# A chosen expert multiplied twice in mid-stage with the same weight pieces, 33 chunks always run

## The chip, the cores and the metric

One core of one Trainium2 chip runs the kernel. The metric is the device time of one execution in microseconds (us); the kernel before takes 1665.71 us, the median of 3 runs (1665.44 to 1667.03). The parts of a core that matter here: TensorE (PE in the profile) multiplies, VectorE (DVE) and ScalarE (ACT) do the elementwise work, GpSimd (POOL) issues gathers, and SyncE (SP) issues every other DMA.

## The reference

Two layers over 512 tokens of 1024 features. Each layer has a mixer (a short convolution in layer 0, sparse attention in layer 1) and then a mixture of experts; the change is in the latter:

```python
g_top = argmax(xf @ w_rg + b_rg)                 # one of 4 groups
e_logits = (xf @ w_re + b_re).reshape(n_tok, 4, 8)
top_vals, top_idx = lax.top_k(e_logits[g_top], 2)
expert = g_top * 8 + top_idx                     # 2 of 32 experts for each token
weights = p_g * softmax(top_vals)
rank = place of the assignment among those of its expert
...
ys = (silu(xc @ w_gate[e]) * (xc @ w_up[e])) @ w_down[e]     # e has 1024x512, 1024x512, 512x1024
out = segment_sum(ys * row_w, row_tok)
```

There are 1024 assignments to 32 experts, so 32 tokens an expert on average; all 32 experts of a layer are used, 6.3 MB of weights each.

## The kernel before

The two expert stages (`experts`, L863) work in chunks of C = 64 tokens of one expert. Chunk c below E = 32 is expert c with its first 64 tokens. An expert with more than 64 gets overflow chunks 32, 33, ...; their number (`novf`) and experts (`ovf_e`) are computed on the chip, and every engine branches on the number after chunk 31 (`overflow`, L1098).

*Weights.* A chunk's weights are 6 pieces of 1 MB: two halves each of gate, up and down (`load_piece`, L433, issued by SP). They lie in a ring of NR = 18 pieces, three chunks. SP loads piece p when the use of piece p - 18 has been counted by the semaphore `s_used` (L1125). Fifteen of the 18 first pieces are prefetched during the stages before, the last three as the first gathered rows land.

*A chunk on TensorE* (`pe_step`, L988): gate-up (`pe_gate_up`, L925), two halves of 16 matmuls, each half after its two pieces have landed; two of the four 128-token tiles of the pair of chunks before, where the weighted results are put back to their tokens by a matmul with a pick matrix (`pe_tile`, L978, `pe_products`, L968); the transpose of the hidden product (L942); the turning of a later pair's rows (`pe_turn`, L915); down (`pe_down`, L952). ACT makes silu (L1013) and y_high (L1021), DVE the hidden product (L1072), y_low (L1051) and the additions into x (L1058). An overflow chunk does all four tiles of what is pending itself, two before the transpose and two before its own down. After the last chunk `end` (L1248) puts back what is left: the pair of chunks 30 and 31 where there was no overflow, the last overflow chunk alone otherwise.

*Tables.* The Router's `vector` ends in `slots` (L762): from the rank and count of every expert it computes the slot (64 x chunk + row) of each assignment. In the expert stage's block `vector_table` (L804) turns slots into one-hot matrices, `tensor_places` (L618) multiplies them into the token list of every chunk, `vector_indices` (L820) makes the gather's indices of it, and `vector_tail` (L830) the weights and the overflow table (`s_table`). The first pair's rows do not wait for this: they have indices of their own (`first_pair`, L750) and are gathered while slots runs.

*Order.* Each engine's queue is in program order. DVE does vector_table, then turns the first rows (`dve_turned`), then vector_indices, vector_tail and the chunks. TensorE turns the first rows, does tensor_places, then the chunks. In chunk 0, after gate-up, it multiplies the weight table (`s_wt`), which SP waits for in layer 1 before it loads the final norm's gain, ahead of piece 18.

Of the kernel before, what the change touches and what calls it, by code (L numbers as in the profile page):

```python
# [59 lines left out]
NCH = E + N_OVF  # L60
# [19 lines left out]
def program(nc, a, out):  # L80
    with ExitStack() as ctx:
# [32 lines left out]
        m.ovf_e = sb("ovf_e", [1, N_OVF + 1], I32)  # L114
        m.banks = ctx.enter_context(nc.psum_tensor("ps", [P, 8, 512], F32))
# [153 lines left out]
def conv_mixer(nc, m, r, hT, u, csb, y):  # L269
# [4 lines left out]
    with ExitStack() as ctx:  # L274
# [9 lines left out]
        rms, rms_row = m.rstd[:, 0, :], sb("c_rms_row", [P, S])  # L284
# [58 lines left out]
        @block.vector  # L343
        def _(dve):
            own = Chain(dve, s_own)

            def roots():
                ms, tmp = m.ss[:, 4:8], m.ss[:, 8:12]
                dve.wait_ge(s_sq, NT)
                dve.tensor_scalar(ms, m.ss[:, 0:4], -0.5 / D, -0.5 * EPS, ALU.mult, ALU.add).then_inc(s_ms, 1)  # L350
                dve.wait_ge(s_rt, 1)
                own.step(dve.reciprocal(rms, rms))

                own.step(dve.tensor_tensor(tmp, rms, rms, ALU.mult))
# [12 lines left out]
            roots()  # L367
            dve.wait_ge(s_row, 1)
            own.step(dve.tensor_copy(rms_row[:], m.ps[6][:]))
            dve.wait_ge(s_cw, 16)  # L370
            for j in range(NK):
                b = j % 2
                dve.wait_ge(s_proj, 3 * j + 1)
                own.step(dve.tensor_tensor(csb[:, b, :], m.ps[3 * b][:], rms_row[:], ALU.mult))
                dve.wait_ge(s_proj, 3 * j + 2)
                own.step(dve.tensor_tensor(csb[:, b, :], csb[:, b, :], m.ps[3 * b + 1][:], ALU.mult))
                own.step(dve.tensor_tensor(u[:, b, 2:], csb[:, b, :], rms_row[:], ALU.mult))
# [5 lines left out]
                own.step(dve.tensor_tensor(y[:, b, :], y[:, b, :], rms_row[:], ALU.mult))  # L383
# [71 lines left out]
class Router:  # L455
# [8 lines left out]
    def __init__(self, nc, m, L, keep, tmp):  # L464
# [13 lines left out]
        self.inc = sb(keep, "inc", [P, E])  # L478
# [17 lines left out]
        self.one, self.base = sb(tmp, "one", [P, E]), sb(tmp, "base", [P, E])  # L496
# [182 lines left out]
    def vector(self, dve):  # L679
# [57 lines left out]
        def constants():  # L737
            own.step(dve.tensor_scalar(self.falling[:], m.iota[:, 0:E], -1.0, 64.0, ALU.mult, ALU.add))
            own.step(dve.memset(self.one[:], -float(C)))
            own.step(dve.tensor_scalar(self.col[:], m.iota[:, 0:NCH], float(C), None, ALU.mult))  # L740
            own.step(dve.tensor_scalar(self.base[:], m.iota[:, 0:E], float(C), None, ALU.mult))
# [20 lines left out]
        def slots():  # L762
# [11 lines left out]
            own.step(dve.scalar_tensor_tensor(out=self.late[:], in0=rank, scalar=float(C) - 0.5, in1=each(begin),  # L774
                                              op0=ALU.is_gt, op1=ALU.mult))
            own.step(dve.tensor_tensor(self.slot[:], rank, each(self.base[:]), ALU.add))
# [53 lines left out]
    def vector_tail(self, dve, own):  # L830
# [11 lines left out]
        own.step(dve.tensor_scalar(self.inc[:], self.inc[:], 1.0 / C, float(1 - E), ALU.mult, ALU.add))  # L842
        own.step(dve.tensor_tensor(self.inc[:], self.inc[:], m.iota[:, 0:E], ALU.add))
# [5 lines left out]
        own.step(dve.tensor_copy(m.ovf_e[:], self.tabf[:]))  # L849
        dve.tensor_copy(m.novf[:], self.inc[0:1, E - 1:E]).then_inc(self.s_table, 1)  # L850
# [12 lines left out]
def experts(nc, m, L, r):  # L863

    with ExitStack() as ctx:
# [32 lines left out]

        def y_place(c):

            return min(c, E - 1) % NY
# [23 lines left out]
        def pe_gate_up(pe, c):  # L925
# [15 lines left out]

# [10 lines left out]
        def pe_down(pe, c):  # L952
# [5 lines left out]
            for h in range(2):  # L958
                p = NPIECE * c + 4 + h
# [138 lines left out]
        def overflow(eng, step, end=None):  # L1098
# [4 lines left out]
            def level(j):  # L1103

                if end:
                    with eng.If(n < j + 1):
                        end(E + j)
                if j < N_OVF:
                    with eng.If(j < n):
                        step(E + j)  # L1110
# [8 lines left out]
        def _(sp):  # L1119
            def step(c):  # L1120
                e = c
                if c >= E:
                    e = sp.value_load(m.ovf_e[0:1, c - E + 1:c - E + 2], min_val=0, max_val=E - 1)
                for p in range(NPIECE * c, NPIECE * (c + 1)):
                    if p >= NR:  # L1125
                        sp.wait_ge(s_used, p - NR + 1)
                        load_piece(sp, m, L, p, e)
# [8 lines left out]
            for c in range(E):  # L1136
                step(c)
# [4 lines left out]
            def end(c):  # L1142
                for n in range(2):
                    sp.wait_ge(s_used, last_use(c, (n,)))
# [15 lines left out]
        def _(act):  # L1160
            for c in range(E):
# [17 lines left out]
        def _(pool):  # L1179
# [4 lines left out]
            for c in range(E):  # L1184
# [11 lines left out]
        def _(dve):  # L1196
# [18 lines left out]
            for c in range(E):  # L1215
# [21 lines left out]
        def _(pe):  # L1237
            for n in range(PAIR):
                pe_turn(pe, n)
            r.tensor_places(pe)  # L1240
            for c in range(E):
                pe_step(pe, c)
# [57 lines left out]
def last_use(c, slots):  # L1300

    return max(p for p in range(NPIECE * c) if ORDER[0][p % NR] in slots) + 1
# [785 lines left out]
```

## Time and profile before

| | |
|---|---|
| median of the runs | 1665.71 us |
| the profiled execution's own time | 1663.04 us |
| its span | 1661.3 us |
| TensorE busy | 1546.8 us, 93% |
| DVE, ACT, POOL busy | 702.1, 308.2, 46.2 us |
| granted TensorE clock, mean | 0.974 |
| moved by DMA | 464.28 MB |
| expert stage of layer 0, of layer 1 | about 259 to 733 us, 1155 to 1655 us |

A line of the profile gives source line, engine, operation, tiles (output <- input), then times. A timeline row is start, duration and count of merged instructions, and in brackets how long the engine stood before it and what released it. "PE clock 1.00" is the full clock, 0.50 half of it. A DMA share of 1 means that all 16 DMA engines were busy.

### The profile page before, as it was taken

How to read it: one execution, taken by the hardware profiler on the slowest of the kernel's cores; microseconds unless marked ns; L12 is line 12 of the kernel's file. 1: busy time of each engine (PE TensorE's matmuls, PEld its weight loads, DVE VectorE, ACT ScalarE, POOL GpSimd, SP SyncE). 2: the span in 40 equal slices, each digit the busy share in tenths (PEclk: the TensorE clock that was granted, in tenths of full speed). 3: DMA queues.
4: the chain of work that ended last, by engine and by line, in shares of the span. 5: the costliest groups of instructions: out<-in, count | busy, mean ns of one | idle time of the engine just before them, and what ended most of it. 6: DMA issues, size and time to landing. Idle time of an engine off the chain costs nothing. (4 is left out here: it accounts for less than half of the span.)

```text
span 1661.3 us, 18728 instructions
## 1 busy us (share of the span) xinstructions
PE 1546.8 (93%) x7356; PEld 725.5 (44%) x7356; DVE 702.1 (42%) x1507; ACT 308.2 (19%) x639; POOL 46.2 (3%) x61
## 2 busy tenths in 40 slices
PE   8999987999999999989999899996999998899995
PEld 4444453444444334345654445554344443433442
DVE  2222344333333233355364599535233333323335
ACT  2000130000000000030333478622000100000002
POOL 0000001000000000000000000000000000000000
PEclk9999998999999999999999999997999999999998
DMA  6271409999999999954310300064999999999993
GB/s 203 76 274 55 169 38 368 418 421 419 420 420 421 420 420 420 419 162 145 102 51 0 152 2 1 10 274 168 383 420 420 420 420 419 421 420 420 420 420 145
DMA packets 112647, 464.28 MB, mean 279 GB/s; under 512 B 29473, under 2 KB 56097, under 8 KB 62625
## 3 DMA queue, kind: packets, MB, share of 16 engines
q1 hardware_dynamic: 107216, 454.52, 68.2%
q0 software_dynamic: 5328, 8.40, 1.4%
q8 instruction: 64, 1.05, 0.3%
q14 instruction: 39, 0.31, 0.1%
HBM read 467.60 MB, written 6.29 MB: 285 GB/s over the span
## 5 line engine op out<-in xcount | busy, mean ns | idle before, releaser
L937 PE MATMUL ps<-raw,e_xT 128*64 128x512 f32 x2080 | 474.5, 604 | 44.3 <-DMA raw<-in_expert_w_up 44.3
L937 PEld LDWEIGHTS ps<-raw,e_xT 128*64 128x64 f32 x2080 | 156.0, 139 | 350.6 <-issue 348.3
L1072 DVE TENSOR_TENSOR e_sg_hid<-e_sg_hid,ps 64x512 f32<-64x512 f32 x65 | 44.3, 681 | 446.9 <-ACT e_sg_hid L1013 446.9
L1058 DVE TENSOR_TENSOR x_res<-x_res,ps 128x512 f32<-128x512 f32 x264 | 168.9, 681 | 3.7 <-PE ps L973 1.6
L407 PE MATMUL ps<-c_hT,raw 128*128 128x512 f32 x384 | 165.2, 592 | 0.4 <-DMA raw<-in_conv_w_in 0.4
L963 PE MATMUL ps<-raw,e_hT 128*64 128x512 f32 x704 | 160.8, 598 | 0.9
L1013 ACT ACTIVATE e_sg_hid<-ps 64x512 f32<-64x512 f32 x65 | 38.6, 593 | 477.8 <-PE ps L937 477.8
L1021 ACT ACTIVATE e_yhi<-ps,e_wtab 128x512 fp32r<-128x512 f32 x65 | 44.7, 687 | 399.4 <-PE ps L963 399.4
L1742 PE MATMUL ps<-a_spare,raw 128*128 128x512 f32 x256 | 115.1, 606 | 3.8 <-DVE a_spare L1503 3.8
L973 PE MATMUL ps<-e_yhi,e_pick 64*128 64x512 f32 x520 | 109.6, 418 | 4.8 <-DVE x_res L1058 3.9
L407 PEld LDWEIGHTS ps<-c_hT,raw 128*128 128x128 f32 x384 | 72.8, 190 | 91.5 <-issue 90.9
L1051 DVE SCALAR_TENSOR_TENSOR e_ylo<-ps,e_wtab,e_yhi 128x512 fp32r<-128x512 f32 x65 | 48.8, 751 | 143.4 <-ACT e_yhi L1021 143.4
L973 PE MATMUL ps<-e_ylo,e_pick 64*128 64x512 f32 x520 | 103.0, 393 | 0.4 <-DVE e_ylo L1051 0.4
L963 PEld LDWEIGHTS ps<-raw,e_hT 128*64 128x64 f32 x704 | 46.6, 136 | 86.6 <-issue 75.4
L973 PEld LDWEIGHTS ps<-e_yhi,e_pick 64*128 64x128 f32 x520 | 48.7, 184 | 66.4 <-issue 52.4
L1742 PEld LDWEIGHTS ps<-a_spare,raw 128*128 128x128 f32 x256 | 49.4, 195 | 63.8 <-issue 63.4
L963 PE MATMUL ps<-e_raw,e_hT 128*64 128x512 f32 x336 | 76.7, 598 | 0.5
L2053 ACT ACTIVATE a_spare<-ps,t_mn 128x128 f32<-128x128 f32 (+3 forms) x128 | 66.6, 528 | 53.4 <-DVE t_mn L2009 52.9
L675 POOL DMA_INDIRECT r_rows<-rows_x,r_idx x37 | 37.8, 1023 | 1008.8 <-PE ps L921 825.7
L921 PE MATMUL ps<-ident,r_rows 128*128 128x128 f32 x276 | 46.6, 295 | 17.4 <-DMA r_rows<-rows_x,r_idx 17.4
L1941 PE MATMUL ps<-a_kT,a_qr 64*128 64x128 f32 (+3 forms) x256 | 52.8, 490 | 6.4 <-ACT a_spare L2053 5.0
L2009 DVE TENSOR_REDUCE t_mn<-ps 128x2 f32<-128x256 f32 (+3 forms) x64 | 52.4, 822 | 7.2 <-PE ps L1947 6.0
(274 smaller groups left out, 1345.3 us busy)
## 6 DMA issues: line engine op xcount, KB each, us to landing
raw<-in_expert_w_gate SPq DMA_DIRECT2D x130, 1024.0 KB, 26.7
raw<-in_expert_w_up SPq DMA_DIRECT2D x130, 1024.0 KB, 27.3
raw<-in_expert_w_down SPq DMA_DIRECT2D x88, 1024.0 KB, 27.1
e_raw<-in_expert_w_down SPq DMA_DIRECT2D x42, 1024.0 KB, 27.7
raw<-in_conv_w_in SPq DMA_DIRECT2D x11, 1024.0 KB, 9.7
raw<-in_w_kv SPq DMA_DIRECT2D x6, 1024.0 KB, 6.4
raw<-in_conv_w_out SPq DMA_DIRECT2D x1, 4096.0 KB, 18.9
raw<-in_attn_w_in SPq DMA_DIRECT2D x4, 1024.0 KB, 5.2
```

What stands on the lines that cost most here:

```text
L407: mm = pe.matmul(m.ps[3 * (j % 2) + i][:], win[:, n % 2, k, c, (j % 2) * P:(j % 2 + 1) * P], hT[:, k, :], start=(k == 0), stop=(k == NK - 1))
L921: tr = pe.transpose(turn_bank(n)[:, k * GS:(k + 1) * GS], rows[:, q % 2, (h * HK + k) * P:(h * HK + k + 1) * P], m.ident[:])
L937: mm = pe.matmul(ps_gu[C - C * i:2 * C - C * i, :], xT[:, q % 2, k, u * C:(u + 1) * C], ring(m, L, p)[:, kk * F:(kk + 1) * F], start=(k == ...
L963: mm = pe.matmul(ps_y[n * C:(n + 1) * C, :], hT[:, 2 * h + kk, :], ring(m, L, p)[:, kk * D + n * 512:kk * D + (n + 1) * 512], start=(h == ...
L973: mm = pe.matmul(banks[n][:], pick[half, pick_place(c), t * P:(t + 1) * P], part[half, y_place(c), :], start=(first and part is yhi), stop ...
L1021: act.activation(yhi[:, y_place(c), :], ps_y[:], ACT.Copy, scale=wtab[:, c:c + 1]).then_inc(s_yhi, 1)
L1051: dve.scalar_tensor_tensor(out=ylo[:, y_place(c), :], in0=ps_y[:], scalar=wtab[:, c:c + 1], in1=yhi[:, y_place(c), :].bitcast(F32), op0=AL ...
L1058: return dve.tensor_tensor(x, x, bank[:], ALU.add).then_inc(done, 1)
L1742: mm = pe.matmul(m.ps[FB[i % 3]][:], wk[:, n % 2, k, (i % 2) * P:(i % 2 + 1) * P], h[:, k, :], start=(x == 0), stop=(x == NK - 1))
L1941: mm = pe.matmul(m.ps[h][:, 0:n], m.qr[rows, (g * HPG + h) // 2, t * P:(t + 1) * P], m.kT[rows, b, g, 0:n], start=True, stop=t >= MASK_T)
L2009: dve.tensor_reduce(mn[:, i % 2, 2 * pair:2 * pair + 2], m.banks[:, 2 * pair:2 * pair + 2, 0:n], AX.X, ALU.min).then_inc(s_mn, 1)
L2053: act.activation(pr[:, i % NB, h, 0:n], m.ps[h][:, 0:n], ACT.Exp, bias=mn[:, i % 2, h:h + 1], scale=-1.0, accum_out=sm[:, i % NB, h:h + 1] ...
```

## The change

Each layer picks one expert of those from number 6 (FIXED) on: the first with more than 64 tokens, or expert 20 (TWICE) if none has. The picked expert and expert 20 swap places; the order is a table, `expert_at`, written by DVE and read by SP from place 6 on. The expert in place 20 is multiplied in two chunks, 20 and 21, its tokens up to the 64th and those beyond it up to the 128th. Both use the pieces of place 20; the pieces come free after the second. Places 21 to 31 become chunks 22 to 32, so 33 chunks (NB) always run on 32 loads. Overflow chunks, for any other expert over 64 and for the picked one over 128, begin at 33. Chunk 32 has the form of an overflow chunk. Further, vector_table moves behind the turned first rows on DVE and tensor_places into chunk 0's gate-up on TensorE, and the convolution stage's root-mean-square row lies in memory that the router uses later.

```diff
-NCH = E + N_OVF
+TWICE = 20
+FIXED = 6
+NB = E + 1
+NCH = NB + N_OVF + 1
...
             def each(x):
                 return x.unsqueeze(1).broadcast_to([P, NT, E])
 
-            own.step(dve.tensor_scalar(ovn, cnt, -(C / 2 + 0.5), MAGIC * C, ALU.add, ALU.add))
+            sel, cap, chunk, perm, experts = self.sel[:], self.cap[:], self.chunk[:], self.perm[:], m.iota[:, 0:E]
+            top, shift = self.c1[:, 2:3], self.c1[:, 3:4]
+
+            own.step(dve.scalar_tensor_tensor(out=cap, in0=cnt, scalar=C + 0.5, in1=self.prior[:], op0=ALU.is_gt, op1=ALU.mult))
+            own.step(dve.scalar_tensor_tensor(out=cap, in0=self.hot[:], scalar=0.25, in1=cap, op0=ALU.mult, op1=ALU.add))
+            own.step(dve.tensor_reduce(top, cap, AX.X, ALU.max))
+            own.step(dve.tensor_scalar(sel, cap, top, None, ALU.is_equal))
...
+            own.step(dve.scalar_tensor_tensor(out=perm, in0=self.hot[:], scalar=shift, in1=perm, op0=ALU.mult, op1=ALU.add))
+            own.step(dve.scalar_tensor_tensor(out=chunk, in0=perm, scalar=TWICE + 0.5, in1=perm, op0=ALU.is_gt, op1=ALU.add))
+            own.step(dve.scalar_tensor_tensor(out=ovn, in0=sel, scalar=-float(C), in1=cnt, op0=ALU.mult, op1=ALU.add))
+            own.step(dve.tensor_scalar(ovn, ovn, -(C / 2 + 0.5), MAGIC * C, ALU.add, ALU.add))
             own.step(dve.tensor_scalar(ovn, ovn, MAGIC * C, 0.0, ALU.subtract, ALU.max))
-            own.step(dve.tensor_tensor_scan(self.inc[:], self.one[:], ovn, float(C * E), ALU.add, ALU.add))
+            own.step(dve.tensor_tensor_scan(self.inc[:], self.zero[:], ovn, float(C * NB), ALU.add, ALU.add))
+            own.step(dve.tensor_scalar(cap, sel, float(C), float(C), ALU.mult, ALU.add))
...
+        def first_piece(c):
+            return NPIECE * (c if c <= TWICE else c - 1)
+
+        def freed(p):
+            return p + 1 if p < NPIECE * TWICE else p + 1 + NPIECE
...
-                pieces = [NPIECE * c + 2 * b + i for i in range(2)]
+                pieces = [first_piece(c) + 2 * b + i for i in range(2)]
...
+                if c == 0 and b == 0:
+                    r.tensor_places(pe)
...
-                p = NPIECE * c + 4 + h
+                p = first_piece(c) + 4 + h
...
+            def load(place, e):
+                for p in range(NPIECE * place, NPIECE * (place + 1)):
+                    if p >= NR:
+                        sp.wait_ge(s_used, freed(p - NR))
+                        load_piece(sp, m, L, p, e)
...
             for c in range(E):
-                step(c)
+                if c == FIXED:
+                    sp.wait_ge(r.s_table, 1)
+                load(c, c if c < FIXED else sp.value_load(m.expert_at[0:1, c:c + 1], min_val=0, max_val=E - 1))
...
-            for c in range(E):
+            for c in range(NB):
                 act_step(act, c)
...
-            own = r.vector_table(dve)
             for n in range(PAIR):
                 dve_turned(dve, n)
+            own = r.vector_table(dve)
             r.vector_indices(dve, own)
...
-            r.tensor_places(pe)
-            for c in range(E):
+            for c in range(NB):
                 pe_step(pe, c)
```

## Rows read from the trace of the kernel before

**Rows 1.** The page's span, and busy us (share of the span) xinstructions of TensorE.
```profile
span 1661.3 us, 18728 instructions
...
PE 1546.8 (93%) x7356; PEld 725.5 (44%) x7356; DVE 702.1 (42%) x1507; ACT 308.2 (19%) x639; POOL 46.2 (3%) x61
```

**Rows 2.** The page's 40 equal slices: GB/s that the DMA engines moved.
```profile
GB/s 203 76 274 55 169 38 368 418 421 419 420 420 421 420 420 420 419 162 145 102 51 0 152 2 1 10 274 168 383 420 420 420 420 419 421 420 420 420 420 145
```

**Rows 3.** Windows: busy us (instructions) of each engine, granted TensorE clock, DMA share, GB/s.
```profile
300.00:480.00 180.00, 179.49 (x952) 76.74 (x954) 71.51 (x121) 16.65 (x26) 6.95 (x7) 1.00 1.01 420
...
480.00:719.00 239.00, 219.29 (x1120) 93.16 (x1118) 80.33 (x135) 20.29 (x32) 6.94 (x7) 0.98 1.01 418
...
1160.00:1172.00 12.00, 11.47 (x84) 4.96 (x82) 4.96 (x15) 0.59 (x1) 2.15 (x2) 1.00 0.82 293
...
1360.00:1633.00 273.00, 248.09 (x1278) 106.06 (x1276) 92.69 (x157) 24.32 (x37) 8.93 (x9) 0.99 1.00 414
```

**Rows 4.** The chain of waits, layer 1's down products: start, us, what.
```profile
1195.32 3.65 PE ps L963 x16
...
1208.93 3.65 PE ps L963 x16
```

**Rows 5.** Timeline of TensorE: start, us, matmuls of half a gate-up [idle before <-releaser].
```profile
547.26 5.35 PE L937 MATMUL ps<-raw,e_xT 128*64 128x512 f32 x16 [2.09 <-DMA raw<-in_expert_w_up]
...
714.91 3.65 PE L937 MATMUL ps<-raw,e_xT 128*64 128x512 f32 x16 [0.85 <-DMA raw<-in_expert_w_up]
...
1612.45 3.65 PE L937 MATMUL ps<-raw,e_xT 128*64 128x512 f32 x16 [1.11 <-DMA raw<-in_expert_w_up]
...
1628.33 3.65 PE L937 MATMUL ps<-raw,e_xT 128*64 128x512 f32 x16 [2.08 <-DMA raw<-in_expert_w_up]
```

**Rows 6.** DMA issues: count, size, median us to landing.
```profile
raw<-in_expert_w_gate SPq DMA_DIRECT2D x130, 1024.0 KB, 26.7
...
r_rows<-rows_x,r_idx POOLq DMA_INDIRECT x37, 8.5
```

**Rows 7.** Windows, the hidden product L1072 alone: DVE busy (count), clock, DMA share, GB/s.
```profile
250.00:735.00 485.00, 21.79 (x32) 0.97 0.98 403
1146.00:1650.00 504.00, 22.48 (x33) 0.98 0.96 397
```

**Rows 8.** Timeline of SP's DMA issues before layer 1's last expert load.
```profile
1586.78 6.79 SPq L439 DMA_DIRECT2D raw<-in_expert_w_down  x2
1595.09 0.71 SPq L439 DMA_DIRECT2D raw<-in_expert_w_gate  x1
```

**Rows 9.** Timeline, ACT's y_high of both last chunks, DVE's last additions of layer 0.
```profile
725.33 0.69 ACT L1021 ACTIVATE e_yhi<-ps,e_wtab 128x512 fp32r<-128x512 f32 x1 [6.12 <-PE ps L963]
...
1641.84 0.69 ACT L1021 ACTIVATE e_yhi<-ps,e_wtab 128x512 fp32r<-128x512 f32 x1 [9.22 <-PE ps L963]
...
727.39 3.86 DVE L1058 TENSOR_TENSOR x_res<-x_res,ps 128x512 f32<-128x512 f32 x6 [0.59 <-PE ps L973]
...
731.67 1.28 DVE L1058 TENSOR_TENSOR x_res<-x_res,ps 128x512 f32<-128x512 f32 x2 [0.42 <-PE ps L973]
```

**Rows 10.** Timeline around the start of layer 1's experts: DVE, then PE, POOL, SP.
```profile
1146.66 0.18 DVE L770 TENSOR_SCALAR r_ovn<-ps 128x32 f32<-128x32 f32 x1
...
1152.05 0.56 DVE L816 TENSOR_TENSOR r_ctok<-r_chot,token 128x384 fp32r<-128x384 f32 x1
1156.64 0.69 DVE L1044 TENSOR_TENSOR e_xT<-ps,r_gp 128x512 f32<-128x512 f32 x1 [4.03 <-PE ps L921]
...
1166.51 0.68 DVE L1072 TENSOR_TENSOR e_sg_hid<-e_sg_hid,ps 64x512 f32<-64x512 f32 x1 [3.18 <-ACT e_sg_hid L1013]
...
1157.11 1.14 PE L627 MATMUL ps<-r_ctok,r_rhot 128*64 128x48 f32 x8
...
1159.67 0.99 POOL L675 DMA_INDIRECT r_rows<-rows_x,r_idx  x1 [11.08 <-DVE r_idx L827]
...
1166.78 0.33 SPq L1140 DMA_DIRECT2D r_coded<-in_norm_final  x1
```

More of the change, by code:

```diff
@@ L368, in _ @@
             dve.wait_ge(s_row, 1)
-            own.step(dve.tensor_copy(rms_row[:], m.ps[6][:]))
+            own.step(dve.tensor_copy(rms_row, m.ps[6][:]))
             dve.wait_ge(s_cw, 16)
@@ L382, in _ @@
                                                       op0=ALU.mult, op1=ALU.add))
-                own.step(dve.tensor_tensor(y[:, b, :], y[:, b, :], rms_row[:], ALU.mult))
+                own.step(dve.tensor_tensor(y[:, b, :], y[:, b, :], rms_row, ALU.mult))
                 dve.wait_ge(s_proj, 3 * j + 3)
@@ L495, in __init__ @@
         self.c1 = sb(tmp, "c1", [P, 4])
-        self.one, self.base = sb(tmp, "one", [P, E]), sb(tmp, "base", [P, E])
+        self.zero, self.prior, self.hot = (sb(tmp, n, [P, E]) for n in ("zero", "prior", "hot"))
+        self.sel, self.cap, self.chunk = (sb(tmp, n, [P, E]) for n in ("sel", "cap", "chunk"))
         self.ovn, self.begin = sb(tmp, "ovn", [P, E]), sb(tmp, "begin", [P, E])
@@ new lines, in slots @@
+            own.step(dve.tensor_reduce(top, cap, AX.X, ALU.max))
+            own.step(dve.tensor_scalar(sel, cap, top, None, ALU.is_equal))
+            own.step(dve.scalar_tensor_tensor(out=perm, in0=experts, scalar=-float(TWICE), in1=sel, op0=ALU.add, op1=ALU.mult))
+            own.step(dve.tensor_reduce(shift, perm, AX.X, ALU.add))
+            own.step(dve.tensor_tensor(perm, experts, perm, ALU.subtract))
+            own.step(dve.scalar_tensor_tensor(out=perm, in0=self.hot[:], scalar=shift, in1=perm, op0=ALU.mult, op1=ALU.add))
@@ L773, in slots @@
+            own.step(dve.tensor_scalar(cap, sel, float(C), float(C), ALU.mult, ALU.add))
             own.step(dve.tensor_tensor(begin, self.inc[:], ovn, ALU.subtract))
-            own.step(dve.scalar_tensor_tensor(out=self.late[:], in0=rank, scalar=float(C) - 0.5, in1=each(begin),
-                                              op0=ALU.is_gt, op1=ALU.mult))
-            own.step(dve.tensor_tensor(self.slot[:], rank, each(self.base[:]), ALU.add))
+            own.step(dve.tensor_tensor(begin, begin, cap, ALU.subtract))
@@ L777, in slots @@
+            own.step(dve.scalar_tensor_tensor(out=begin, in0=chunk, scalar=-float(C), in1=begin, op0=ALU.mult, op1=ALU.add))
+            own.step(dve.tensor_tensor(self.late[:], rank, each(cap), ALU.is_ge))
+            own.step(dve.tensor_tensor(self.late[:], self.late[:], each(begin), ALU.mult))
+            own.step(dve.scalar_tensor_tensor(out=self.slot[:], in0=each(chunk), scalar=float(C), in1=rank, op0=ALU.mult, op1=ALU.add))
             own.step(dve.tensor_tensor(self.slot[:], self.slot[:], self.late[:], ALU.add))
@@ L840, in vector_tail @@
                           .broadcast_to([P, NTK, NCH]), ALU.mult).then_inc(self.s_cw, 1)
-        own.step(dve.tensor_scalar(self.inc[:], self.inc[:], 1.0 / C, float(1 - E), ALU.mult, ALU.add))
-        own.step(dve.tensor_tensor(self.inc[:], self.inc[:], m.iota[:, 0:E], ALU.add))
+        own.step(dve.tensor_scalar(self.inc[:], self.inc[:], 1.0 / C, -float(NB), ALU.mult, ALU.add))
         own.step(dve.tensor_tensor(self.tab, self.inc[0:1, :].unsqueeze(1).broadcast_to([1, N_OVF, E]),
@@ L849, in vector_tail @@
         own.step(dve.tensor_copy(m.ovf_e[:], self.tabf[:]))
+        own.step(dve.tensor_copy(m.expert_at[:], self.perm[0:1, :]))
         dve.tensor_copy(m.novf[:], self.inc[0:1, E - 1:E]).then_inc(self.s_table, 1)
@@ L1106, in level @@
                     with eng.If(n < j + 1):
-                        end(E + j)
+                        end(NB + j)
                 if j < N_OVF:
                     with eng.If(j < n):
-                        step(E + j)
+                        step(NB + j)
                         level(j + 1)
@@ L1119, in _ @@
         def _(sp):
-            def step(c):
[L1121 to L1127, printed above, removed]
+            def load(place, e):
[3 more added lines that the diff above has]
+                        load_piece(sp, m, L, p, e)
+            def step(c):
+                j = c - NB
+                load(E + j, sp.value_load(m.ovf_e[0:1, j + 1:j + 2], min_val=0, max_val=E - 1))
             sp.wait_ge(r.s_rows[0], 16)
@@ L1208, in last_add @@
                 dve_sum(dve, t, n, ps_c[t % 2][n], s_sum)
-            own = r.vector_table(dve)
             for n in range(PAIR):
                 dve_turned(dve, n)
+            own = r.vector_table(dve)
             r.vector_indices(dve, own)
             r.vector_tail(dve, own)
-            for c in range(E):
+            for c in range(NB):
                 dve_step(dve, c)
@@ L1239, in _ @@
                 pe_turn(pe, n)
-            r.tensor_places(pe)
-            for c in range(E):
+            for c in range(NB):
                 pe_step(pe, c)
@@ L1297, in kv_weight, with last_piece @@
     return w.rearrange("(k p) c -> p k c", p=P)[:, :, c:c + n]
-def last_use(c, slots):
-    return max(p for p in range(NPIECE * c) if ORDER[0][p % NR] in slots) + 1
+def last_piece(c, slots):
+    return max(p for p in range(NPIECE * (c - 1)) if ORDER[0][p % NR] in slots)
 def feature_weights(sp, m, n):
```

17 lines of the change are left out of this document (10 added, 7 removed).

## The prediction

> **What bounds the kernel now.** I read the page's busy table first: TensorE is busy 93% of a 1661.3 us span [rows 1], which alone would say that a 33rd chunk in each layer costs time. The slices correct that [rows 2]: in both expert stages (slices 8 to 17 and 30 to 39 of 40) the DMA engines move a flat 420 GB/s. So two resources are nearly level, and the windows say which leads where [rows 3]. In the first part of layer 0's stage (300 to 480 us) TensorE is busy 179.49 of 180.00 us, at the full clock: it lives on the 18 prefetched pieces and sets its own pace. In the later part (480 to 719, 1360 to 1633 us) it is busy 219.29 of 239.00 and 248.09 of 273.00 us while the DMA share stays at 1.01 and 1.00: the weights set the pace. What TensorE waits for there is a piece of expert_w_up, 0.85 to 2.09 us at a time [rows 5].
>
> The two paces come from the timeline. When TensorE leads, a chunk's down product starts 13.61 us after the last one's (1195.32 to 1208.93) [rows 4]. When the weights lead, the second half of gate-up starts as its piece lands: in layer 0 the 21st chunk's at 547.26 and the 32nd's at 714.91, 11 periods of 15.24 us [rows 5]. TensorE has thus 1.63 us in hand per chunk there.
>
> How many chunks there are now: 130 pieces of w_gate at two per chunk make 65 [rows 6], and the windows with the hidden product alone show 32 in layer 0 and 33 in layer 1 [rows 7]. So one expert in layer 1 has over 64 tokens and is loaded a second time. Which it is stands in no row; routing the reference's own inputs gives it: expert 22 with 85 tokens in layer 1, and none over 64 in layer 0 (the fullest has 48). 22 is past the sixth and 85 is under 128, so the table swaps it to place 20, and the two chunks there hold all its tokens.
>
> **The change part by part.**
>
> *Loads.* Layer 1 loads 32 experts instead of 33, layer 0 still 32. The end of the weight stream sets the end of a stage, so layer 1's moves forward by one period. The last interval of layer 1 itself, 1612.45 to 1628.33, is 15.88 [rows 5], but its last pieces land while the queue runs dry, as layer 0's last do too; I take one average period: **-15.2 us**, and the two as ends.
>
> *The second chunk of place 20, and whether TensorE catches up.* Both layers now run 33 chunks on 32 loads. Chunk 21 has its weights there already, so it costs TensorE 13.61 us and the stream nothing, and TensorE falls 13.61 us behind. From the second half of chunk 20 to that of the last chunk there are 12 periods of TensorE, 12 x 13.61 = 163.3 us, against 11 of the stream, 167.65. It is level again some three chunks before the end, with 4.3 us in hand, and from there the weights lead. A chunk in which the clock was halved for a while took 5.35 us for its half of gate-up instead of 3.65 [rows 5], 1.7 more; two of these fit into the margin. So the extra chunk costs **0** in its place, hidden under the weight loads of places 21 to 31; without that cover it would cost up to 13.61 in each layer.
>
> *The held pieces.* Place 20's six pieces come free only in chunk 21, one chunk later, and the loads of place 23 wait for them on SP. A piece takes 27 us from issue to landing [rows 6], against the 2.5 that one piece needs at 15.24/6, so some 10 pieces are queued ahead of it, and SP's issues, 6.79 us for two, mostly wait for room in the queue [rows 8]. A hold of 13.61 us leaves 13 us of queue: **0**; if it were not covered it would cost up to 13.61 less the queue.
>
> *SP's new work.* From place 6 on SP reads a register per place. The trace has one such read, before the last place of layer 1: the issues before it end at 1593.57, the next begins at 1595.09 [rows 8], 1.5 us per chunk, hidden behind the same 27 us of queue: 0. That load's address comes from a register, and its first issue took 0.71 us, no more than others. The wait for the table at place 6 stands before pieces that chunk 3 frees, three chunks or some 40 us after the table is there: 0.
>
> *The last chunk.* Chunk 32 now always takes the overflow form: four tiles of the pair before it instead of two, in the chunk. ACT, whose work on y_high waits for all of it, sat idle 9.22 us before it in the last chunk of layer 1 and 6.12 in that of layer 0 [rows 9]. Layer 0 pays the difference, **+3.1**; layer 1 had that form already. Behind it only one chunk's products are left: layer 0's eight last additions spread from 727.39 to 732.95 [rows 9], 5.56 us, with a gap for TensorE; at 0.64 each they take 5.1: **-0.4**. The next stage's key weights wait for place 30's pieces, now used in chunk 31, by then nearly level; the slice behind the stage moves only 162 GB/s [rows 2], so the load has room: 0.
>
> *The router.* slots() grows by 14 DVE instructions, mostly 128x32, at 0.18 us or somewhat more each [rows 10]: 2.5 to 3.5 us. slots() and vector_table ran from 1146.66 to 1152.61, and then DVE idled 4.03 us until the first gathered rows were turned at 1156.64 [rows 10]; vector_table also moves behind the turned rows, so the end comes no later than now: 0.
>
> *Chunk 0.* The places table (1157.11, 1.14 us) moves from ahead of the gate-up into its middle. The gate-up starts 0.7 us sooner, and the table's inputs are ready some 2.5 us after the turned rows, at about 1160.7, when the first half of gate-up is nearly done: at its end little or nothing is gained. But the indices of pairs 1 and 2, which the gather of 1159.67 waits for, come about 4 us later, and behind them DVE's tail, which ran from about 1158.2 to 1163.33 (3.18 us before the hidden product), now ends near 1167.4, where the hidden product started at 1166.51 [rows 10]. TensorE loses 1 to 3 us in chunk 0. Does the stream? In layer 1 SP stands until the weight table and issues the norm gain at 1166.78 [rows 10], then piece 18; the weight table still comes right after gate-up, so this stays. The pause of the stream there is 12 x (1 - 293/420) = 3.6 us [rows 3], and the two gathers fell into it; now they compete with weights. **+0.5 us per layer, +1.0**, an estimate; ends: -0.7 each (the earlier start carried through) and +4 each (the gathers, now 4 us later and 8.5 us to landing [rows 6], stall chunk 0 and the stream with it).
>
> The sum: -15.2 + 3.1 - 0.4 + 1.0 = **-11.5 us**. Of the profiled span that makes 1661.3 - 11.5 = 1649.8, with 1.7 around it (its own time is 1663.0) 1651.5. The median of the runs, 1665.71, stands 2.7 above the profiled one; carried over, **1654.2 us**.
>
> One rule of the Trainium skill speaks of the price of a load: "DMA: Bandwidth & Descriptors", Specifications, gives an HBM limit of about 358 GB/s per core. The windows show 420 [rows 3], so the trace disagrees and decides. By the page's figure a period would be 15.24 x 420/358 = 17.9 us and the sum, as an estimate, -14.2 us.
>
> **The rivals.**
>
> *The ring starves (slower).* If the queue held less than the hold, because SP is not as far ahead at place 20 as the median says, the stream would stop in both layers for x us, and TensorE, behind as well, could not win it back: -11.5 + 2x. At x = 13.61 that is +15.7, 1681 us; it is slower than before from x = 5.8. For it: SP stood 6.79 us on two issues, so it is not always ahead. Against: 27 us to landing and 420 GB/s throughout. 0.05.
>
> *TensorE does not quite catch up.* Place 31 then ends late by 2 to 4 us per layer: more half-clock stretches, or a chunk pace over 167.65/12 = 13.97. The clock is 0.98 and 0.99 in the later windows [rows 3], in stretches with waits; the waits go. -11.5 + 6 gives 1660. 0.15.
>
> *Chunk 0 stalls.* Late gathers delay the second pair by 3 to 4 us and the stream with it: 1654 + 7 = 1661. The queue of the first pieces speaks against it. 0.10.
>
> *The start or the tail gives more.* The earlier gate-up carries through (-1.4 instead of +1.0) and the last additions hide the four tiles: 1654.2 - 2.4 - 2.7 = 1649.1. 0.10.
>
> *The change doesn't catch the expert.* The second load stays, layer 1 has 34 chunks on 33 loads, and layer 0 pays +2.7: 1669.4 with the start's 1.0, slower. The counts above speak against it. 0.02.
>
> The forecast has 0.58: 1651 to 1656.5 for itself. The range for 8 in 10 takes in most of the catch-up and chunk-0 cases: 1649 to 1661. A measurement here tells 0.2%, 3.3 us, from no change: faster is below 1662.4. Forecast, more, and most of the two part-losses make 0.88; the rest of these 0.06 for the same; starving and not catching 0.06 for slower.
>
> **What would show it.** The step on loads: 128 pieces of w_gate and 6.3 MB less. The catch-up: in both layers no wait for expert_w_up from chunk 21 for some nine chunks, periods of 13.61, then waits again before the last; if there are none before the last chunk, TensorE never caught up. The hold: the DMA share stays at 1.01 through chunks 20 to 24. The last chunk: 9.2 us from the hidden product to y_high in both layers. The router: no DVE work between the last slot and the turned rows that delays the latter. The forecast is wrong if the stream pauses at place 20, if its pause in chunk 0 grows, or if the stages other than the expert ones move by over 1 us.

## The result, and the profile after

The changed kernel takes 1653.92 us, the median of 4 runs (1651.47 to 1655.6), against 1665.58 for the kernel before on the same chip: 0.9933 of its time, 95% interval 0.9921 to 0.9945, or 11.7 us less. In a second comparison it was 1653.35 against 1665.05 (0.9926, 0.9914 to 0.9938), again 11.7 us less. 1654.2 was forecast.

The page of the profiled execution (its own time 1655.6 us, the longest of the four), which answers to [rows 1, 2, 6]:

```profile
span 1653.9 us, 19530 instructions
...
PE 1560.3 (94%) x7428; PEld 730.9 (44%) x7428; DVE 715.5 (43%) x1550; ACT 308.2 (19%) x640; POOL 46.8 (3%) x62
...
GB/s 204 77 266 64 169 26 344 420 421 419 421 420 420 421 421 420 421 199 164 77 55 23 153 2 1 1 271 82 345 421 420 420 420 421 421 420 421 420 420 149
...
raw<-in_expert_w_gate SPq DMA_DIRECT2D x128, 1024.0 KB, 25.6
```

TensorE has more work (1560.3 us against 1546.8) in a shorter span. 128 pieces of w_gate are loaded and not 130, and the flat 420 GB/s of both stages has stayed. The windows, with the hidden product alone (first fence) and with all engines (second), answer to [rows 7] and [rows 3]:

```profile
250.00:742.00 492.00, 22.49 (x33) 0.97 0.97 397
1154.00:1650.00 496.00, 22.49 (x33) 0.97 0.95 393
```

```profile
480.00:558.00 78.00, 72.89 (x382) 31.98 (x380) 29.62 (x51) 6.40 (x10) 2.96 (x3) 0.98 1.01 421
558.00:700.00 142.00, 141.59 (x750) 60.30 (x748) 55.62 (x94) 13.50 (x21) 4.95 (x5) 1.00 1.01 420
700.00:721.00 21.00, 18.93 (x100) 7.83 (x96) 5.73 (x10) 1.85 (x3) 0.99 (x1) 1.00 0.99 396
```

33 chunks in each layer. From 558 to 700 us TensorE is busy 141.59 of 142.00 us and the DMA share is 1.01 all the same: both are saturated at once, which in the kernel before they never were in this part. The half gate-ups of layer 0 show where that begins and ends (start, us, instructions [idle before <-releaser]), answering to [rows 5]:

```profile
549.24 5.35 PE L968 MATMUL ps<-raw,e_xT 128*64 128x512 f32 x16 [2.25 <-DMA raw<-in_expert_w_up]
561.13 7.04 PE L968 MATMUL ps<-raw,e_xT 128*64 128x512 f32 x32
...
701.76 3.65 PE L968 MATMUL ps<-raw,e_xT 128*64 128x512 f32 x16 [0.89 <-DMA raw<-in_expert_w_up]
...
716.73 3.65 PE L968 MATMUL ps<-raw,e_xT 128*64 128x512 f32 x16 [1.17 <-DMA raw<-in_expert_w_up]
```

Chunk 20's second half still waited 2.25 us for its piece, and ran in part at half clock (5.35 us for 16 matmuls instead of 3.65). Chunk 21 follows without a wait, its 32 matmuls in one piece; its second half starts 15.3 us after chunk 20's, which is a period of 13.61 and the 1.7 us of the half clock. So do all up to chunk 30, at 13.61 us. The wait comes back at 701.76, in chunk 31, the last but one. TensorE was one chunk late and has caught up. In layer 1 chunk 20's half ran at the full clock, and the wait was back sooner, in chunk 29:

```profile
1575.78 3.65 PE L968 MATMUL ps<-raw,e_xT 128*64 128x512 f32 x16 [0.56 <-DMA raw<-in_expert_w_up]
```

Two distances put the span together: from the issue of a layer's first gather to its last hidden product, and what lies between. Both are differences of rows like [rows 10] and of the last L1072 or L1105 row:

| us | before | after | second profile |
|---|---|---|---|
| layer 0, first gather to last hidden product | 467.6 | 469.1 | 468.4 |
| layer 0, last hidden product to last addition's end | 13.7 | 17.3 | 17.0 |
| layer 0's last addition to layer 1's first gather | 414.6 | 416.6 | 414.7 |
| layer 1, first gather to last hidden product | 485.1 | 470.0 | 470.2 |
| layer 1, last hidden product to the end | 28.7 | 29.0 | 28.2 |
| span | 1661.3 | 1653.9 | 1650.4 |

The gain is the fourth row, -15.1 us; the losses are the first two. The third, where the change touches next to nothing, differs by 1.9 us between two profiles of the same kernel; the mean granted clock in that stretch was 0.96 in the first of them and 0.97 in the second. So the span of a single profile (-7.4 and -10.9) tells less than the median of the runs.

### The profile page after: what moved, and what is told of

Same layout as the page of the kernel before. It is cut to its first block and busy times, and to the rows that moved or that the text cites. A ratio compares the mean times of both kernels' runs of the same rounds, so it can differ in the third digit from the quotient of the medians.

```text
span 1653.9 us, 19530 instructions
## 1 busy us (share of the span) xinstructions
PE 1560.3 (94%) x7428; PEld 730.9 (44%) x7428; DVE 715.5 (43%) x1550; ACT 308.2 (19%) x640; POOL 46.8 (3%) x62
## 5 line engine op out<-in xcount | busy, mean ns | idle before, releaser
L1105 DVE TENSOR_TENSOR e_sg_hid<-e_sg_hid,ps 64x512 f32<-64x512 f32 x66 | 45.0, 681 | 410.3 <-ACT e_sg_hid L1046 410.0
L1091 DVE TENSOR_TENSOR x_res<-x_res,ps 128x512 f32<-128x512 f32 x272 | 173.9, 681 | 4.3 <-PE ps L1006 2.1
L996 PE MATMUL ps<-e_raw,e_hT 128*64 128x512 f32 x352 | 80.4, 598 | 0.7
## 6 DMA issues: line engine op xcount, KB each, us to landing
raw<-in_expert_w_gate SPq DMA_DIRECT2D x128, 1024.0 KB, 25.6
```

The lines of the kernel that those rows point to most:

```text
L996: mm = pe.matmul(ps_y[n * C:(n + 1) * C, :], hT[:, 2 * h + kk, :], ring(m, L, p)[:, kk * D + n * 512:kk * D + (n + 1) * 512], start=(h == ...
L1091: return dve.tensor_tensor(x, x, bank[:], ALU.add).then_inc(done, 1)
```

## The experiments

Differences are to the changed kernel, each by way of the kernel before on the same chip (a ratio has an interval of about 0.0015, 2.5 us, to each side, so a difference between two kernels has 3 us and more). The last column is worked out from the medians; by the ratios some rows come out up to 1.5 us elsewhere, hold_two_chunks at 0.

| kernel | us | ratio to before, interval | to the changed one |
|---|---|---|---|
| after_same_chip | 1653.35 | 0.9926 (0.9914 to 0.9938) | |
| order_back | 1652.39 | 0.9923 (0.9911 to 0.9935) | -1.0 |
| no_overflow_load | 1647.29 | 0.9887 (0.9873 to 0.9901) | -6.1 |
| twice_12 | 1652.88 | 0.9921 (0.9901 to 0.9941) | -0.2 |
| twice_24 | 1661.69 | 0.9968 (0.9953 to 0.9982) | +6.4 |
| twice_28 | 1673.55 | 1.0053 (1.0039 to 1.0068) | +20.2 |
| hold_two_chunks | 1653.79 | 0.9926 (0.991 to 0.9943) | -1.5 |
| hold_three_chunks | 1672.42 | 1.0043 (1.0026 to 1.0059) | +19.3 |
| short_last_chunk | 1647.78 | 0.9889 (0.9873 to 0.9906) | -7.5 |
| small_loads_later | 1643.5 | 0.9858 (0.9842 to 0.9875) | -11.8 |
| gains_in_first_stage | 1641.36 | 0.9855 (0.9839 to 0.9872) | -11.7 |
| late_tables_again | 1647.89 | 0.9898 (0.9881 to 0.9914) | -5.2 |

The second profile of the changed kernel, used in the table above and in some comparisons below, is after_same_chip, with no edit:

> The changed kernel again, on the chip of the other runs of this group. My theory: about 11.7 us under the kernel before (ratio 0.993), the same as in the first comparison.

### The price of a load: no_overflow_load

The kernel before, with the number of overflow chunks set to 0, so that the 21 tokens of expert 22 beyond its 64th are left out.

> The kernel before with the number of overflow chunks set to zero, so that the 21 tokens beyond the 64th of layer 1's expert 22 are left out. It takes away layer 1's second load, its 33rd chunk and nothing else. Theory A (the weight stream sets the end): -15.2 for the period of 6 pieces and -2.7 for the shorter form of the last chunk, together about -18 us against the kernel before. Theory B (the chunk is worth its TensorE time): -13.6 - 2.7 = -16.3 or less.

```diff
-        dve.tensor_copy(m.novf[:], self.inc[0:1, E - 1:E]).then_inc(self.s_table, 1)
+        dve.tensor_scalar(m.novf[:], self.inc[0:1, E - 1:E], 0.0, None, ALU.mult).then_inc(self.s_table, 1)
```

Measured -17.8 us against the kernel before. The interval of the ratio, 16.5 to 21.1 us, barely leaves out theory B's 16.3; the profile decides for theory A. Layer 1's distance from first gather to last hidden product fell from 485.1 to 469.8 us, by 15.3 and not 13.6, and what lies behind it from 28.7 to 25.8. The changed kernel's distance, with a chunk more on as many loads, is 470.0. In the rows of ACT's last y_high (as [rows 9]) the short form stands against the changed kernel's, which has the long one in both layers:

```profile
1627.60 0.69 ACT L1021 ACTIVATE e_yhi<-ps,e_wtab 128x512 fp32r<-128x512 f32 x1 [6.12 <-PE ps L963]
```

```profile
712.18 0.69 ACT L1054 ACTIVATE e_yhi<-ps,e_wtab 128x512 fp32r<-128x512 f32 x1 [6.12 <-PE ps L996]
...
730.24 0.69 ACT L1054 ACTIVATE e_yhi<-ps,e_wtab 128x512 fp32r<-128x512 f32 x1 [9.22 <-PE ps L996]
```

6.12 us before y_high in the usual chunk, 9.22 in chunk 32: 3.1 us, as forecast.

### Does TensorE win back 1.63 us per chunk? twice_28, twice_24, twice_12

The changed kernel with the doubled place elsewhere, 28, 24 or 12:

```diff
-TWICE = 20
+TWICE = 28
```

It was expected:

> The changed kernel with the doubled place moved from 20 to 28. Theory A (TensorE wins back 1.63 us per chunk from the stream): 3 chunks are left to win back, so each stage ends 13.61 - 3 x 1.63 = 8.7 us late, together +17.4 us against the changed kernel, 1671 us. Theory B (the second chunk is hidden wherever it stands, as the 30 chunks before it leave the pieces loaded): 0.

> The changed kernel with the doubled place moved from 20 to 24. Theory A (TensorE wins back 1.63 us per chunk): 7 chunks are left, 13.61 - 7 x 1.63 = 2.2 us late per stage, so 4.4 us above the changed kernel, 1658 us. Together with place 28 (8.7 us late, 1673.6 measured) and 20 (0) it draws the line. Theory B (what place 28 lost had to do with the end of the stage and not with winning back): 0.

> The changed kernel with the doubled place moved from 20 to 12, where TensorE still sets the pace. Theory A (all that counts is that enough chunks follow: 9 or more): 0, or up to 2 us less, since winning back is done long before the end. Theory B (in the part where TensorE leads, a second chunk costs its 13.61 us): 27 us above.

The last two gate-ups of layer 0 with place 28, and then with place 24:

```profile
706.73 7.04 PE L968 MATMUL ps<-raw,e_xT 128*64 128x512 f32 x32
720.34 7.04 PE L968 MATMUL ps<-raw,e_xT 128*64 128x512 f32 x32
```

```profile
700.43 7.04 PE L968 MATMUL ps<-raw,e_xT 128*64 128x512 f32 x32
714.05 7.04 PE L968 MATMUL ps<-raw,e_xT 128*64 128x512 f32 x32
```

No wait is left: TensorE is late to the end in both. The price is 0, 0, 6.4 and 20.2 us for places 12, 20, 24 and 28, where 0, 0, 4.4 and 17.4 were expected. From 24 to 28 it rises by 13.8 us in two layers, 1.7 a chunk and layer, near the 1.63 of [rows 4, 5]. Both priced places lie 1.2 us per layer higher than worked out, which is within the interval of a difference. The profiles, against after_same_chip, place it: with place 28 the distance to the last hidden product is 7.7 us longer in layer 0 and 8.9 in layer 1 (8.7 expected), with place 24 it is 1.5 and 6.0 longer (2.2 expected). In the last of these the half gate-up of chunk 24 itself ran in part at half clock, 1.7 us more:

```profile
1515.53 5.35 PE L968 MATMUL ps<-raw,e_xT 128*64 128x512 f32 x16 [2.26 <-DMA raw<-in_expert_w_up]
```

Theory B fell in each. Place 12 lies in the part where TensorE leads: the second chunk isn't free there either, it delays the meeting with the stream and not the end. The first wait for a piece of w_up comes in chunk 27 of layer 0, at 638.50 us, and in the kernel before in chunk 16, at 485.99.

### Does the held ring starve? hold_two_chunks, hold_three_chunks

> The changed kernel in which SP waits one chunk longer for every piece from place 20 on, so that the ring is two places deep there instead of three; nothing else is changed. The arithmetic and the loads are the same. Theory A (some 10 pieces, 27 us, are queued ahead, and the hold of the change takes 13.61 of it): the second hold takes the rest, the queue runs nearly dry, and the time is 0 to 3 us above the changed kernel. Theory B (the ring starves as soon as the hold is there): 13 us or more per stage, 26 in all, above it.

> The changed kernel in which SP waits two chunks longer for every piece from place 20 on, so that the ring is one place deep there; the loads and the arithmetic are the same. Theory A (the stream starves only when the hold is deeper than the queue; two chunks of hold measured 0): now the stream cannot run ahead of TensorE by more than six pieces, so it stands still while place 20 is multiplied again, and each stage ends up to 13.6 us later, 20 to 27 us above the changed kernel. Theory B (the depth of the ring doesn't matter in this part at all): within 3 us of it.

```diff
-            return p + 1 if p < NPIECE * TWICE else p + 1 + NPIECE
+            return p + 1 if p < NPIECE * TWICE else p + 1 + 2 * NPIECE                         # two
+            return p + 1 if p < NPIECE * TWICE else min(p + 1 + 3 * NPIECE, NPIECE * NB)       # three
```

Windows behind chunk 20 of layer 0, first of two chunks of hold, then of three:

```profile
565.00:580.00 15.00, 14.95 (x84) 6.75 (x84) 6.04 (x11) 1.88 (x3) 0.99 (x1) 1.00 1.00 411
580.00:595.00 15.00, 14.96 (x87) 6.97 (x83) 6.29 (x11) 1.28 (x2) 0.00 (x0) 1.00 1.01 424
```

```profile
565.00:580.00 15.00, 14.95 (x82) 6.28 (x80) 5.73 (x10) 1.28 (x2) 0.99 (x1) 1.00 0.95 393
580.00:595.00 15.00, 14.96 (x82) 6.33 (x80) 4.94 (x8) 1.58 (x3) 0.00 (x0) 1.00 0.22 72
595.00:610.00 15.00, 13.81 (x76) 5.97 (x74) 5.73 (x10) 1.34 (x3) 0.99 (x1) 1.00 1.01 423
```

With two chunks the stream only dips to 411 GB/s and the time is the same; with three it stops (72 GB/s in 15 us, while TensorE is busy 14.96 of them) and the distances to the last hidden product are 10.7 and 10.2 us longer than in after_same_chip. Theory A both times, though the 19.3 us are just under the lower end of its 20 to 27. From 550 to 610 us the stream moved 327 GB/s instead of 420, which is 13.3 us of work; why only 10.7 us of it show at the end is not settled. The rival of the prediction is a real mechanism with its edge two chunks away from the change.

### The order of the tables: order_back

> The changed kernel with DVE's vector_table ahead of the turned rows again and TensorE's tensor_places ahead of chunk 0 again. Theory A (the late gather of pairs 1 and 2 delays chunk 0 and thins the weight stream there): the first hidden products of layer 0 come some 5 us earlier relative to the first gather, the stream loses 1 to 2 us less at each start, and the time is 1 to 3 us below the changed kernel's. Theory B (the order costs nothing because the stream sets the pace): within 0.7 us of it. Theory C (the order was needed, since slots() is longer now): 1 us or more above it.

```diff
+            own = r.vector_table(dve)
             for n in range(PAIR):
                 dve_turned(dve, n)
-            own = r.vector_table(dve)
...
+            r.tensor_places(pe)                 # ahead of chunk 0, no longer inside it
```

1.0 us less, which the runs can't tell from nothing, so theory B is not excluded by the time. The profile can tell the local effect. Layer 1, changed kernel, then order_back:

```profile
1154.86 1.01 POOL L680 DMA_INDIRECT r_rows<-rows_x,r_idx  x1 [64.88 <-DVE r_idx L767]
1171.80 0.99 POOL L680 DMA_INDIRECT r_rows<-rows_x,r_idx  x1 [15.92 <-DVE r_idx L850]
```

```profile
1150.98 1.01 POOL L680 DMA_INDIRECT r_rows<-rows_x,r_idx  x1 [64.89 <-DVE r_idx L767]
1163.36 0.99 POOL L680 DMA_INDIRECT r_rows<-rows_x,r_idx  x1 [11.37 <-DVE r_idx L850]
```

The second gather comes 16.9 us after the first in the changed kernel and 12.4 here (12.1 before, [rows 10] and the first gather at 1147.58), the first hidden product 20.7 against 19.1 us after it. From first gather to last hidden product layer 0 took 467.5 and layer 1 469.2, 0.9 and 1.0 less than in after_same_chip. Theory A holds for the place of the effect, and for its size 0.9 to 1 per layer in one pair of profiles. Its 5 us in layer 0 did not come: the first hidden product was 1.7 us earlier after the first gather (19.6 against 21.3), the second 3.4. Theory C fell. The pair shows one thing more: order_back has the second chunk of place 20 without the late tables, and its layer 0, with 33 chunks on 32 loads, took 467.5 us where the kernel before took 467.6 with 32 chunks.

### Towards a better version: short_last_chunk, small_loads_later, gains_in_first_stage

> The kernel with the order of tables put back (order_back), and in which, where there is no overflow, the last chunk is put back to its tokens together with chunks 30 and 31 in one accumulation: the first two tiles' share of 30 and 31 before its transpose, everything else behind its down product. Theory A (the four tiles of the overflow form cost 3.1 us ahead of down): y_high of the last chunk starts 3.1 us sooner after the hidden product, the additions behind it take about 1 us longer, together 2.2 us less per layer, 4.4 less than order_back, 1648 us. Theory B (the additions on DVE set the tail, and they only move): within 1 us of order_back.

```diff
+            def last_chunk():                          # TensorE, where there is no overflow
+                pe_gate_up(pe, E)
+                pe.wait_ge(s_pick, E)
+                pe.wait_ge(s_ylo, E)
+                for t in range(2):
+                    pe.wait_ge(s_add, 2 * (LAST - 1 + t))
+                    for u in (E - 2, E - 1):
+                        pe_products(pe, u, (yhi, ylo), t, ps_c[t], u == E - 2)
+                pe_transpose(pe, E)
+                pe_down(pe, E)
+                end(NB)                                # its unit is (E - 2, E - 1, E)
```

ACT and DVE get the matching branch, y of chunk 32 a place of its own, and its pick matrix the memory of rhot.

```profile
725.13 0.69 ACT L1060 ACTIVATE e_yhi<-ps,e_wtab 128x512 fp32r<-128x512 f32 x1 [6.05 <-PE ps L1002]
```

```profile
727.20 2.48 DVE L1102 TENSOR_TENSOR x_res<-x_res,ps 128x512 f32<-128x512 f32 x4 [0.59 <-PE ps L1012]
731.41 1.29 DVE L1102 TENSOR_TENSOR x_res<-x_res,ps 128x512 f32<-128x512 f32 x2 [1.72 <-PE ps L1012]
733.96 1.29 DVE L1102 TENSOR_TENSOR x_res<-x_res,ps 128x512 f32<-128x512 f32 x2 [1.26 <-PE ps L1012]
```

6.05 us and not 9.22 before y_high: the 3.1 us are back. Behind it DVE now waits for TensorE (1.72 and 1.26 us in front of the last two pairs of additions), and in this layer that takes all of it again: from the last hidden product to the last addition's end layer 0 took 16.1 us in order_back and 16.1 here, where part of it ran at half clock (mean granted clock 0.90, in order_back 1.00). In layer 1 the tail fell from 28.6 to 25.5 us. By the ratios it is 5.7 us under order_back, 4.4 were expected; the spans differ by 3.5. So the profiles show the gain in layer 1 alone, and what it is worth in layer 0 at the full clock is not shown.

The rest are built on short_last_chunk. In it the small loads of SP were moved: layer 0's two gains, 4 KB each, and in layer 1 the final norm's gain, which SP issues only after waiting for the weight table.

> The kernel short_last_chunk with the small loads (the two gains of layer 0's end, the final norm's gain of layer 1) issued at place 8 and not ahead of piece 18. Theory A (SP stands there and the weight stream pauses, so each us of pause is a us of the stage): the pause shrinks by 2 to 3 us in each layer, 4 to 6 us less than short_last_chunk, 1643 us. Theory B (the pause is that of the freed pieces, not of SP): within 1 us of short_last_chunk.

```diff
-            if L == 0:
-                with nc.allow_non_contiguous_dma(reason="small vectors"):
-                    sp.dma_start(m.kv_scale[:, 0, :], m.a["norm_kv"].rearrange("(k p) -> p k", p=P)).then_inc(m.kv_gain, 16)
-                    sp.dma_start(m.kv_scale[:, 1, :], m.a["norm_mix"][1].rearrange("(k p) -> p k", p=P)).then_inc(m.kv_gain, 16)
             for c in range(E):
...
+                if L == 0 and c == 8:
+                    with nc.allow_non_contiguous_dma(reason="small vectors"):
+                        sp.dma_start(m.kv_scale[:, 0, :], m.a["norm_kv"].rearrange("(k p) -> p k", p=P)).then_inc(m.kv_gain, 16)
+                        sp.dma_start(m.kv_scale[:, 1, :], m.a["norm_mix"][1].rearrange("(k p) -> p k", p=P)).then_inc(m.kv_gain, 16)
-                if L and c == 2:
+                if L and c == 8:
```

4.3 us less on the same chip: theory A in sum, with theory B's 1 us near the lower end of the interval. But the two layers differ. In layer 1 the stream moved 376 GB/s from 1150 to 1190 us and 353 in short_last_chunk: 40 x 23/420 = 2.2 us won. In layer 0 what was won in front went again at place 8:

```profile
344.61 0.43 SPq L1192 DMA_DIRECT2D kv_scale<-in_norm_kv  x1
345.08 15.34 SPq L1193 DMA_DIRECT2D kv_scale<-in_norm_mix  x1
361.17 3.31 SPq L443 DMA_DIRECT2D raw<-in_expert_w_gate  x1
```

```profile
345.00:370.00 25.00, 24.92 (x136) 10.93 (x134) 10.18 (x18) 1.87 (x3) 0.99 (x1) 1.00 0.94 358
```

SP stands 15.34 us at the second load of 4 KB, and the stream falls to 358 GB/s for 25 us, 3.7 us lost for the two loads.

small_loads_later with layer 0's two gains loaded in the convolution stage, and no longer at place 8:

> The kernel small_loads_later with layer 0's two small gains loaded in the convolution stage, right behind the first six expert pieces, where the DMA engines are idle. At place 8 they cost the stream of layer 0 as much as ahead of piece 18 (3.6 us, measured). Theory A (the 2048 four-byte pieces are work for the DMA engines wherever the stream is full): 3.6 us less, 1640 us. Theory B (layer 0's stage has another limit): within 1 us of 1643.5.

```diff
             prefetch(sp, m, 0, range(NPIECE))
+            with nc.allow_non_contiguous_dma(reason="small vectors"):
+                sp.dma_start(m.kv_scale[:, 0, :], m.a["norm_kv"].rearrange("(k p) -> p k", p=P)).then_inc(m.kv_gain, 16)
+                sp.dma_start(m.kv_scale[:, 1, :], m.a["norm_mix"][1].rearrange("(k p) -> p k", p=P)).then_inc(m.kv_gain, 16)
             sp.wait_ge(s_proj, 3 * NK)
```

The same 25 us of layer 0 are now full:

```profile
345.00:370.00 25.00, 24.91 (x136) 10.92 (x134) 9.99 (x17) 2.04 (x4) 0.99 (x1) 1.00 1.01 421
```

1641.36 us, the lowest of all, 23.4 under the kernel before; by the ratios (0.9855 and 0.9858) it can't be told from small_loads_later. In the profiles layer 0's stage, first gather to last addition, is 1.5 us shorter than there and not 3.6; the middle is 0.8 longer. Which theory holds stays open.

### The order once more: late_tables_again

gains_in_first_stage, in which the tables' order is that of the kernel before, with the changed kernel's order put back in:

> The kernel gains_in_first_stage with the order of the change put in again: vector_table behind the turned rows on DVE, tensor_places inside chunk 0's gate-up on TensorE. Theory A (the late gather and the late tail delay chunk 0 by 2 to 5 us, and what is freed late pauses the stream, which SP no longer hides): 1 to 3 us above gains_in_first_stage. Theory B (the stream doesn't notice): within 0.7 us.

```diff
             for n in range(PAIR):
                 dve_turned(dve, n)
+            own = r.vector_table(dve)                    # from ahead of the loop
...
+                if c == 0 and b == 0:
+                    r.tensor_places(pe)                  # from ahead of chunk 0
```

6.5 us above gains_in_first_stage, more than theory A said. Layer 1's chunk 0 in TensorE's timeline, here and, below, in gains_in_first_stage:

```profile
1172.43 0.69 PE L993 MATMUL ps<-ident,e_sg_hid 64*128 64x64 f32 x4 [1.46 <-DVE e_sg_hid L1122]
1175.98 1.12 PE L964 MATMUL ps<-ident,r_rows 128*128 128x128 f32 x4 [2.86 <-DMA r_rows<-rows_x,r_idx]
1177.02 5.77 PE L1008 MATMUL ps<-raw,e_hT 128*64 128x512 f32 x16
```

```profile
1172.17 0.65 PE L964 MATMUL ps<-ident,r_rows 128*128 128x128 f32 x4
1172.83 3.65 PE L1006 MATMUL ps<-raw,e_hT 128*64 128x512 f32 x16
```

Down starts at 1177.02 instead of 1172.83 behind 2.86 us of waiting for the gathered rows, and from 1160 to 1190 us the stream moves 351 GB/s against 410, 4.2 us less work done. The pieces that take the place of chunk 0's down pieces are issued at 1180.75 instead of 1174.81. The loss is layer 1's: its distance from first gather to last hidden product grew by 5.2 us (466.1 to 471.4), layer 0's by 1.5 (466.1 to 467.5), and layer 0's tail was 1.5 shorter.

In the changed kernel the same order cost 1.0 us in layer 1. There SP issues nothing until the weight table is there (1171.62 in after_same_chip), and the rows of pairs 1 and 2 are gathered from 1168.51 on; here it issued four pieces from 1165.92 on, around the gather of 1167.91. The time that these two gathers of layer 1 took to land, in after_same_chip and then here:

```profile
DMA to landing us min/median/max: 3.3/3.9/4.5
```

```profile
DMA to landing us min/median/max: 8.0/9.3/10.7
```

So the late gather landed in time where SP stood. That this and the late pieces make up the whole difference is argued from these rows and not tested.

## Why the prediction was right

*Bound.* That the weight stream and not TensorE's 93% sets the end is shown from both sides: a chunk without a load costs nothing (no_overflow_load against the changed kernel, 469.8 and 470.0 us in layer 1; the kernel before against order_back, 467.6 and 467.5 in layer 0), and a stream stopped for 13.3 us costs 10.7 and 10.2 (hold_three_chunks).

*Loads, -15.2.* -15.1 in layer 1's distance in the changed kernel, which holds its loss in chunk 0 too; -15.3 in no_overflow_load.

*Catching up, 0.* Right. The forecast had TensorE level some three chunks before the end. In layer 0 the wait returned in chunk 31, with two chunks in hand: over the 11 periods from 549.24 to 701.76 TensorE had 2.8 us more time than 11 x 13.61 (11 chunks on 10 loads), and the half clock of chunk 20 took 1.7 of them. In layer 1, without it, the wait was back in chunk 29. The price of places 24 and 28 lies 1.2 us per layer above the sum. What these are is not settled: a half-clock half accounts for 1.7 us in one of the four stages, the interval could hold them all, and no run takes the half-clock halves away.

*Held pieces and SP's reads, 0.* Right; the second chunk of hold was free too. SP's reads were not tested alone; the stream ran at 420 GB/s beside them.

*Last chunk, +3.1 - 0.4.* The 3.1 stands in the rows. Layer 0's tail grew by 3.6 and 3.3 in the two profiles of the changed kernel, in both of which the clock was at half for part of the tail (mean 0.90), and by 2.4 in order_back (13.7 to 16.1), where it was not (1.00).

*Router, 0.* Right: slots took 6.2 us in layer 1 instead of 2.8, and DVE still idled 4.21 us ahead of the first turned rows, where it had idled 4.03 [rows 10]. With vector_table back ahead of them (order_back) 0.92 us were left.

*Chunk 0, +1.0.* The sum was right within what can be told: order_back gives 1.0. The picture was not. TensorE was to lose 1 to 3 us in chunk 0; first hidden product and the step to the second together lost 5.2 us in layer 0 (2.1 + 3.1) and 3.4 in layer 1 (1.8 + 1.6). The hidden product stood behind DVE's tail: TensorE waited 1.61 and 1.46 us for it, and 0.52 in the kernel before. Behind it the down products ran partly at half clock, and in layer 0 of this one profile the rows of pair 1 landed late:

```profile
276.44 1.12 PE L952 MATMUL ps<-ident,r_rows 128*128 128x128 f32 x4 [1.50 <-DMA r_rows<-rows_x,r_idx]
...
1177.60 5.26 PE L996 MATMUL ps<-raw,e_hT 128*64 128x512 f32 x16
```

That little of it reached the end in layer 1 was, as far as the rows of late_tables_again tell, the shelter of SP's stop, named in the prediction for the front but not as what covers the gather. Without it the price is 6.5 us (late_tables_again), near the prediction's outer end of 8 for the pair of layers.

*Rivals.* The starving ring was ruled out by hold_two_chunks; the unfinished catch-up by the waits that returned; the stall of chunk 0 happened, mostly on TensorE alone. The change caught the expert: 33 chunks in layer 1 without an overflow.

*Luck.* That 1654.2 met 1653.92 so closely is in part luck, since the measurement is only good for 2 us to each side. The parts fit the profiles within about 1 us each. One of the prediction's own signs of being wrong did appear in one profile: the stretch between the expert stages was 2.0 us longer, in the other 0.1.

*The skill's figure.* By the 358 GB/s of the Trainium skill ("DMA: Bandwidth & Descriptors", Specifications) one place would take 17.9 us, an estimate; the page's row derives the figure as half of the 716 GB/s that two cores share, and one core runs here. The runs show 15.1, at 420 GB/s.

## What to carry to other kernels

Where two resources are nearly level, ask which ends last in each part, and what one of them has in hand per step: work added to the other one was free where enough steps followed to win it back, and cost more with every step that was missing. A reordering that costs nothing may be sheltered by another stall beside it; when that stall is removed, try the order again. Hold a buffer as long as the queue ahead of it lasts and no longer: here two chunks were free and the third cost 10 us in each stage.

## What the runs showed of the hardware

Two loads of 4 KB, each in 1024 pieces of four bytes, took 3.7 us from a full weight stream (358 GB/s instead of 421 over 25 us), as much as 1.6 MB of weights, and the second held SP 15.34 us; ahead of piece 18 the same load held it 6.12 (short_last_chunk). In the changed kernel's profile a gather of rows landed in 8.3 us (median of 38) while weight pieces stood in the other queue, and these took 25.6.
